# Sliding-window attention with the values stationary, alternating head groups and an early division

## The chip, the cores and the metric

The kernel runs on one core of one Trainium2 chip. The metric is the time of one execution on the device in microseconds (us); lower is better. A core has five engines, each with its own queue of instructions in strict program order: TensorE (PE in the profile; PEld is its weight loads), VectorE (DVE), ScalarE (ACT), GpSimd (POOL) and SyncE (SP, which here issues the loads of weights). They meet only at semaphores: an instruction waits until a counter has reached a value, and another engine's instruction raises that counter.

## The reference

Two layers over 256 tokens of width 1024. Each layer has a mixer (a gated linear recurrence, HGRN2, beside a sliding-window attention), then a dense or an expert MLP, then a gated embedding. The change concerns the attention:

```python
CHUNK = 64; SW_HEADS = 8; KV_HEADS = 2; GROUP = 4; HEAD_DIM = 64; WINDOW = 128

def swa_mixer(q, k, v, q_gain, k_gain, sinks):
    q = rms_norm(q.reshape(B, S, SW_HEADS, HEAD_DIM), q_gain) * HEAD_DIM ** -0.5
    k = rms_norm(k.reshape(B, S, KV_HEADS, HEAD_DIM), k_gain)
    ...
    s = jnp.einsum('bnqhgd,bnkhd->bnhgqk', qb, kb)      # own chunk and the one before
    s = jnp.where(valid, s, -jnp.inf)
    probs = softmax(concatenate([s, sink], -1))[..., :-1]
    o = jnp.einsum('bnhgqk,bnkhd->bnqhgd', probs, vb)
    return o.reshape(B, S, SW_WIDTH)

merged = sigmoid(gate_a) * (ya @ w_pa) + sigmoid(gate_b) * (yb @ w_pb)
x = x + merged @ w_o
```

Everything is float32. Query heads 0 to 3 use key-value head 0, heads 4 to 7 use key-value head 1. The output is (1, 256, 1024).

## The kernel before, in words

**Weights.** All large products are split in two parts for accuracy. A weight unit is 128 x 2048 numbers. SP loads it into one of 6 `raw` slots, ACT writes its high part `w_hi` (L530), DVE its low part `w_lo` (L786), each into one of 3 slots; PE makes three products of it: high by high, low by high, high by low (L1293 to L1295), 512 columns each. `keep_up(used)` on ACT and on DVE splits all units up to number `used + 2`; where it is called decides where in the queue of its engine a unit is split. The units of a mixer are numbered from `base`: 0 to 18 the input projection (`IN_UNITS` = 19; 11 to 18 are the gates, two units to each of `GATES` to `GATES + 3`), 19 and 20 `w_pa`, 21 and 22 `w_pb`, 23 to 26 `w_o`.

**The order of work** is written out by hand for each engine, in three functions named `mixer`, one for ACT, one for DVE and one for PE. No scheduler changes it. The recurrence is done in nine levels: `level_product(g)` on PE, `level_step(g)` on DVE, `level_exp(j)` on ACT. The attention lies between them and between the units of the gates.

**The attention** goes in three tasks, `TASKS`: token tile 0 with all 8 heads, token tile 1 with heads 0 to 3, token tile 1 with heads 4 to 7. Token tile 0 has 128 keys, tile 1 has 256 (the two tiles, masked). Each task fills 1024 columns: 8 heads by 128 keys or 4 by 256. A task goes through these steps:

1. PE, `attention_scores`: one product per head. Both operands lie on 64 partitions, 0 to 63 for heads of group 0 and 64 to 127 for heads of group 1. It raises `sw_scores`.
2. DVE, `softmax_max`: mask, maximum, sink (L921 to L926).
3. ACT, `softmax_exp`: one exponential per head, with its sum (L582 to L585). It raises `sw_probs`.
4. PE, `flip_probs`: 8 transposes of 128 x 128 (L1403).
5. ACT, `take_probs`: a copy into `sw_pT` (L592).
6. PE, `attention_out`: for each head and key block a product with the transposed probabilities stationary (128 x 128) and the values moving (64 columns), so the result has tokens on partitions.
7. DVE, `attention_norm`: sum with the sink, reciprocal (L933, L934), and the multiplication of the result (L937) into `qkv`, which takes the place of the queries. It raises `yb_ready`.

Small products of the attention and of the levels all go through one helper (L1298). Of each such float32 product the trace has two records of PE.

**The end of the mixer.** PE multiplies by the first unit of `w_pa`, then transposes the attention's result by 8 transposes (L1492), then goes on with the second unit of `w_pa`. ACT and DVE split that transposed result into `hT` (L641, L792), PE multiplies by `w_pb`, and DVE merges both branches (L1041 to L1050).

## Time and profile before

| | before |
|---|---|
| median of 3 runs | 1718.02 us (1716.61 to 1719.48) |
| the profiled execution | 1716.82 us, its span 1714.9 us |
| PE, PEld | 1674.0 us (98%), 1389.7 us (81%) |
| DVE, ACT, POOL | 1334.2 us (78%), 1093.1 us (64%), 55.5 us (3%) |
| granted TensorE clock, mean | 0.992 |
| mixer of layer 0, attention part | 101 to 163 us of the span |

Durations of single instructions come from the profiled execution. Its time is 1.2 us below the median, and its span, from the first to the last instruction, 1.9 us below its own time. A busy share is a mean over stages with different limits; whether a saved microsecond counts is read from the waits of the stage in which it lies. Ends of PE instructions are modelled, and one overlaps the next; the time from one start to the next is the better measure. The granted clock is a share of 2.4 GHz; 0.5 is 1.2 GHz.

### The profile page before, as it was taken

The page shows a single profiled execution, that of the slowest core. Times are in us where ns is not written, and L with a number is a line of the kernel's source. Part 1 is how long each engine was busy: PE and PEld are TensorE (multiplying, and loading weights), DVE is VectorE, ACT ScalarE, POOL GpSimd, SP SyncE. Part 2 cuts the span into 40 slices and gives each one's busy share as a digit, 9 for nine tenths or more (in the row PEclk, how much of TensorE's full clock was granted, in tenths as well). Part 3 has the DMA queues.
Part 4 walks back from the last instruction along what each step waited for, and adds up shares of the span by engine and source line. Part 5 has one row for each costly group of instructions (what it writes and reads, how often), then busy time and mean ns, then how long its engine had stood idle before and what let it go on. Part 6 is the DMA issues. An engine that isn't in the chain of part 4 may idle for free.

```text
span 1714.9 us, 20962 instructions
## 1 busy us (share of the span) xinstructions
PE 1674.0 (98%) x7899; PEld 1389.7 (81%) x7899; DVE 1334.2 (78%) x1093; ACT 1093.1 (64%) x897; POOL 55.5 (3%) x52
## 2 busy tenths in 40 slices
PE   7999899999999998999999999999999999999997
PEld 6888788888778887888888888888888888888886
DVE  6785644545567856788988998999998999889885
ACT  5555344344455553777877877778778778778774
POOL 0100000000001000010000000000000000000000
PEclk9999999999999999899999999999999999999999
DMA  8433555565364335599999999999999999999990
GB/s 307 167 123 123 172 172 192 176 196 192 117 213 147 123 123 184 191 363 374 358 380 366 350 383 353 373 377 347 373 385 341 379 377 347 382 377 347 376 370 25
DMA packets 199549, 472.60 MB, mean 276 GB/s; under 512 B 8592, under 2 KB 11216, under 8 KB 199504
## 3 DMA queue, kind: packets, MB, share of 16 engines
q1 hardware_dynamic: 197936, 466.20, 75.6%
q0 software_dynamic: 1568, 5.77, 1.0%
q8 instruction: 32, 0.52, 0.1%
q14 instruction: 13, 0.11, 0.0%
HBM read 469.84 MB, written 2.10 MB: 275 GB/s over the span
## 4 chain that ended last, share of the span: by engine, by line
PE 86%; DVE 9%; issue 3%; ACT 2%; DMA 0%; SPq 0%; DVEq 0%; ACTq 0%
PE ps L1293 26%; PE ps L1295 26%; PE ps L1294 26%; DVE w_lo L786 5%; PE ps L1298 5%; PE ps L1622 1%; ACT w_hi L530 1%; DVE y_lo L1236 1%; DVE hT_lo L792 0%; ACT hT_hi L546 0%; PE ps L1542 0%; PE ps L1403 0%; ACT inner_hi L697 0%; DVE hT_lo L844 0%; PE ps L1384 0%
## 5 line engine op out<-in xcount | busy, mean ns | idle before, releaser
L786 DVE TENSOR_TENSOR w_lo<-raw,w_hi 128x2048 fp32r<-128x2048 f32 x442 | 1007.6, 2290 | 246.7 <-ACT w_hi L530 242.3
L530 ACT ACTIVATE w_hi<-raw 128x2048 fp32r<-128x2048 f32 x442 | 846.5, 1919 | 374.7 <-PE ps L1295 365.1
L1293 PE MATMUL ps<-w_hi,hT_hi 128*128 128x512 f32 (+1 forms) x1600 | 631.2, 394 | 10.9 <-DVE hT_lo L844 4.6
L1295 PE MATMUL ps<-w_hi,hT_lo 128*128 128x512 f32 (+1 forms) x1600 | 621.8, 389 | 0.0
L1294 PE MATMUL ps<-w_lo,hT_hi 128*128 128x512 f32 (+1 forms) x1600 | 621.2, 388 | 0.0
L1293 PEld LDWEIGHTS ps<-w_hi,hT_hi 128*128 128x128 f32 x1600 | 301.7, 189 | 77.3 <-DVE w_lo L786 6.0
L1295 PEld LDWEIGHTS ps<-w_hi,hT_lo 128*128 128x128 f32 x1600 | 301.4, 188 | 63.0
L1294 PEld LDWEIGHTS ps<-w_lo,hT_hi 128*128 128x128 f32 x1600 | 302.0, 189 | 58.8
L1293 PE MATMUL ps<-w_hi,inner_hi 128*128 128x512 f32 x608 | 240.3, 395 | 1.6 <-DVE inner_lo L792 1.6
L1295 PE MATMUL ps<-w_hi,inner_lo 128*128 128x512 f32 x608 | 237.8, 391 | 0.0
L1294 PE MATMUL ps<-w_lo,inner_hi 128*128 128x512 f32 x608 | 237.8, 391 | 0.0
L1293 PEld LDWEIGHTS ps<-w_hi,inner_hi 128*128 128x128 f32 x608 | 114.7, 189 | 26.9 <-DVE inner_lo L792 1.8
L1295 PEld LDWEIGHTS ps<-w_hi,inner_lo 128*128 128x128 f32 x608 | 114.7, 189 | 24.5
L1294 PEld LDWEIGHTS ps<-w_lo,inner_hi 128*128 128x128 f32 x608 | 114.8, 189 | 23.3
L792 DVE TENSOR_TENSOR inner_lo<-ps,inner_hi 128x512 fp32r<-128x512 f32 x72 | 48.8, 685 | 28.4 <-ACT inner_hi L663 14.0
L1298 PE MATMUL ps<-arena 128*128 128x128 f32 (+2 forms) x384 | 50.4, 286 | 1.2 <-DVE arena L937 1.2
L1298 PEld LDWEIGHTS ps<-arena 128*128 128x128 f32 (+1 forms) x384 | 46.9, 191 | 4.3 <-DVE arena L937 1.4
L570 ACT ACTIVATE arena<-ps,rstd 128x512 f32<-128x512 f32 (+1 forms) x40 | 24.4, 661 | 36.8 <-PE ps L1295 36.8
L1206 DVE SCALAR_TENSOR_TENSOR arena<-arena,slot_now,ps 128x512 f32<-128x512 f32 x56 | 41.5, 741 | 0.0
L697 ACT ACTIVATE inner_hi<-ps 128x512 fp32r<-128x512 f32 x56 | 33.1, 591 | 9.9 <-PE ps L1622 9.9
L577 ACT ACTIVATE arena<-arena 128x1024 f32<-128x1024 f32 x16 | 16.7, 1054 | 30.9 <-DVE arena L862 30.9
L1622 PEld LDWEIGHTS ps<-ident,arena 128*128 128x128 f32 x224 | 27.6, 139 | 7.4 <-DVE arena L1206 0.3
(230 smaller groups left out, 776.2 us busy)
## 6 DMA issues: line engine op xcount, KB each, us to landing
raw<-in_w_moe_gate SPq DMA_DIRECT2D x112, 1024.0 KB, 6.9
raw<-in_w_moe_up SPq DMA_DIRECT2D x112, 1024.0 KB, 7.3
raw<-in_w_moe_down SPq DMA_DIRECT2D x112, 1024.0 KB, 6.7
raw<-in_w_in SPq DMA_DIRECT2D x38, 1024.0 KB, 5.6
raw<-in_w_dense_gate SPq DMA_DIRECT2D x14, 1024.0 KB, 5.0
raw<-in_w_dense_up SPq DMA_DIRECT2D x14, 1024.0 KB, 5.1
raw<-in_w_dense_down SPq DMA_DIRECT2D x14, 1024.0 KB, 4.8
raw<-in_w_o SPq DMA_DIRECT2D x8, 1024.0 KB, 4.8
```

The source lines that it names most:

```text
L530: nc.scalar.activation(w_hi[:, n % SLOTS, :], raw[:, n % RAW_SLOTS, :], ACT.Copy).then_inc(high_ready, 1)
L570: nc.scalar.activation(dst(t), src, func, scale=rstd[:, t:t + 1]).then_inc(proj_taken, 1)
L697: nc.scalar.activation(innerT[0][:, :, s % 2 * P:(s % 2 + 1) * P], banks(TRA).rearrange("p (k t) -> p k t", k=4), ACT.Copy).then_inc(item_ ...
L786: nc.vector.tensor_tensor(w_lo[:, n % SLOTS, :], raw[:, n % RAW_SLOTS, :], w_hi[:, n % SLOTS, :].bitcast(F32), ALU.subtract).then_inc(low_ ...
L792: return nc.vector.tensor_tensor(part[1][cols], full, part[0][cols].bitcast(F32), ALU.subtract)
L1206: nc.vector.scalar_tensor_tensor(act[s % 2], act[s % 2], slot_now[:, 0:1], banks(UP), ALU.mult, ALU.mult).then_inc(item_act, 1)
L1236: nc.vector.tensor_tensor(y_lo[:, cols], banks(half), y_hi[:, cols].bitcast(F32), ALU.subtract).then_inc(item_y_split, 1)
L1293: nc.tensor.matmul(o, x_parts[0][x_cols], parts[0], start=first, stop=False)
L1294: nc.tensor.matmul(o, x_parts[0][x_cols], parts[1], start=False, stop=False)
L1295: return nc.tensor.matmul(o, x_parts[1][x_cols], parts[0], start=False, stop=last)
L1298: return nc.tensor.matmul(o, lhsT, rhs, start=start, stop=stop)
L1622: last = nc.tensor.transpose(banks(TRA)[:, k * P:(k + 1) * P], act[s % 2][:, k * P:(k + 1) * P], ident[:, :])
```

## The change

1. `TASKS` now names the heads of each task: task 1 has heads 0, 1, 4, 5 and task 2 heads 2, 3, 6, 7, so each has two heads of either group. `attention_scores` issues a head of group 0, then one of group 1, and so on, each group into its own bank of PSUM.
2. `attention_scale` on DVE takes the sum and the reciprocal and multiplies the probabilities (128 x 1024) before they are transposed; `flip_probs` waits for its semaphore, `sw_scaled`, in place of `sw_probs`.
3. `attention_out` has the values stationary (64 columns) and the probabilities moving (256 columns in task 0, 128 in tasks 1 and 2). The result has head dimensions on partitions, the even head of a pair on 0 to 63 and the odd on 64 to 127: it is already transposed.
4. `take_heads` copies it into the place of the queries. The 8 transposes and `yb_transposed` go; ACT waits for `yb_ready` and for the input projection's end, and ACT and DVE split from SBUF.

```diff
-    TASKS = [(0, 0, 8), (1, 0, 4), (1, 4, 4)]
+    TASKS = [(0, 0, [0, 1, 2, 3, 4, 5, 6, 7]), (1, 0, [0, 1, 4, 5]), (1, 4, [2, 3, 6, 7])]
...
+                act_e.wait_ge(yb_ready, len(TASKS) * (layer + 1))
+                act_e.wait_ge(units_used, base + IN_UNITS)
                 for h in range(2):
-                    act_e.wait_ge(yb_transposed, 2 * layer + h + 1)
-                    nc.scalar.activation(hT[0][:, 2 * h:2 * h + 2, :], banks(GATE + h).rearrange("p (h t) -> p h t", h=2),
-                                         ACT.Copy).then_inc(ybT_high, 1)
+                    nc.scalar.activation(yT(hT[0][:, 2 * h:2 * h + 2, :]), yb[:, 2 * h:2 * h + 2], ACT.Copy).then_inc(ybT_high, 1)
...
-            def attention_norm(layer, a):
+            def attention_scale(layer, a):
...
+                sv = sw_s.rearrange("p (h k) -> p h k", h=heads)
                 dve.wait_ge(sw_probs, len(TASKS) * layer + a + 1)
                 link(nc.vector.tensor_tensor(sw_total[:, hs], sw_sum[:, hs], sw_sink[:, hs], ALU.add))
                 link(nc.vector.reciprocal(sw_recip[:, hs], sw_total[:, hs]))
+                nc.vector.tensor_tensor(sv, sv, sw_recip[:, hs].unsqueeze(2).to_broadcast([P, heads, 1024 // heads]),
+                                        ALU.mult).then_inc(sw_scaled, 1)
+
+            def take_heads(layer, a):
+
                 dve.wait_ge(sw_out, len(TASKS) * layer + a + 1)
...
+                nc.vector.tensor_copy(dst, src).then_inc(yb_ready, 1)
...
                 keep_up(base + 13)
+                attention_scale(layer, 0)
                 level_step(layer, 7)
-                attention_norm(layer, 0)
+                take_heads(layer, 0)
...
                 keep_up(base + 15)
+                attention_scale(layer, 1)
...
-                attention_norm(layer, 1)
+                take_heads(layer, 1)
                 softmax_max(layer, 2)
                 keep_up(base + 16)
+                attention_scale(layer, 2)
                 keep_up(base + 17)
...
             def attention_scores(layer, a):
-                t, h0, heads = TASKS[a]
+                t, _, order = TASKS[a]
                 keys = (t + 1) * P
-                for h in range(h0, h0 + heads):
-                    kv0 = (h // 4) * HEAD_DIM
-                    last = mm(banks(2, 2)[:, (h - h0) * keys:(h - h0 + 1) * keys],
-                              qbT[kv0:kv0 + HEAD_DIM, h % 4, t * P:(t + 1) * P], kbT[kv0:kv0 + HEAD_DIM, 0:keys], True, True)
+                half = len(order) // KV_HEADS
+                for n in range(half):
+                    for v in range(KV_HEADS):
+                        h, slot = order[v * half + n], v * half + n
+                        rows_of = slice(v * HEAD_DIM, (v + 1) * HEAD_DIM)
+                        last = mm(banks(2, 2)[:, slot * keys:(slot + 1) * keys],
+                                  qbT[rows_of, h % 4, t * P:(t + 1) * P], kbT[rows_of, 0:keys], True, True)
                 last.then_inc(sw_scores, 1)
...
-                pe.wait_ge(sw_probs, len(TASKS) * layer + a + 1)
+                pe.wait_ge(sw_scaled, len(TASKS) * layer + a + 1)
...
-                for h in range(heads):
-                    v0 = SW + KV + ((h0 + h) // 4) * HEAD_DIM
+                probs = sw_pT.rearrange("p (b v c j k) -> p b v j c k", b=t + 1, v=KV_HEADS, j=2, k=P)
+                into = banks(OUT_BANK[a]).rearrange("p (v c k) -> p v c k", v=KV_HEADS, c=2)
+                if a:
+                    into = into[:, :, a - 1:a]
+                for v in range(KV_HEADS):
+                    v0 = SW + KV + v * HEAD_DIM
                     for kb in range(t + 1):
-                        last = mm(banks(OUT_BANK[a])[:, h * HEAD_DIM:(h + 1) * HEAD_DIM],
-                                  sw_pT[:, (kb * heads + h) * P:(kb * heads + h + 1) * P],
-                                  qkv[:, kb, v0:v0 + HEAD_DIM], kb == 0, kb == t)
+                        for j in range(2):
+                            last = mm(into[j * HEAD_DIM:(j + 1) * HEAD_DIM, v], qkv[:, kb, v0:v0 + HEAD_DIM],
+                                      probs[:, kb, v, j], kb == 0, kb == t)
                 last.then_inc(sw_out, 1)
...
-                pe.wait_ge(yb_ready, len(TASKS) * (layer + 1))
-                for k in range(4):
-                    for t in range(TILES):
-                        last = nc.tensor.transpose(banks(GATE, 2)[:, k * SEQ + t * P:k * SEQ + (t + 1) * P],
-                                                   qkv[:, t, k * P:(k + 1) * P], ident[:, :])
-                    if k % 2:
-                        last.then_inc(yb_transposed, 1)
```

DVE's queue around the division of task 0, before. `w_lo` is the low part of weight unit 15 (then of unit 16), L886 to L899 are `level_step(7)`, and L933 to L937 are `attention_norm(0)`.

```order
L786 TENSOR_TENSOR w_lo<-raw,w_hi 128x2048 [waits high_ready]
L886 TENSOR_TENSOR arena<-arena 128x4x128 [waits level_exps]
L887 TENSOR_TENSOR arena<-arena 128x4x128
L899 COPY_PREDICATED arena<-masks,ps 128x1024 [waits level_taken,level_scores]
L933 TENSOR_TENSOR sw_total<-sw_sum,sw_sink 128x8 [waits sw_probs]
L934 RECIPROCAL sw_recip<-sw_total 128x8 [waits vector_step]
L937 TENSOR_TENSOR arena<-ps,sw_recip 128x512 [waits sw_out,vector_step]
L786 TENSOR_TENSOR w_lo<-raw,w_hi 128x2048 [waits high_ready]
```

The same place after the change (its lines have other numbers: L791 is the low part, L891 to L904 the level step).

```order
L791 TENSOR_TENSOR w_lo<-raw,w_hi 128x2048 [waits high_ready]
L947 TENSOR_TENSOR sw_total<-sw_sum,sw_sink 128x8 [waits sw_probs]
L948 RECIPROCAL sw_recip<-sw_total 128x8 [waits vector_step]
L949 TENSOR_TENSOR normed<-normed,sw_recip 128x1024 [waits vector_step]
L891 TENSOR_TENSOR arena<-arena 128x4x128 [waits level_exps]
L892 TENSOR_TENSOR arena<-arena 128x4x128
L904 COPY_PREDICATED arena<-masks,ps 128x1024 [waits level_taken,level_scores]
L958 COPY arena<-ps 128x512 [waits sw_out]
L791 TENSOR_TENSOR w_lo<-raw,w_hi 128x2048 [waits high_ready]
```

Sum and reciprocal have moved ahead of the level step, the multiplication has moved with them and is now of the probabilities (`normed` holds them), and all three stand behind the low part of unit 15.

PE's queue from the last level product before the transposes of task 0, before: L1298 is the level product, L1403 the transposes, L1293 the next product of the gates.

```order
L1298 MATMUL ps<-arena 128x128 [waits level_ready,level_taken]
L1298 MATMUL ps<-arena 128x128 x7
L1403 MATMUL ps<-ident,normed 128x128 [waits sw_probs]
L1403 MATMUL ps<-ident,normed 128x128 x7
L1293 MATMUL ps<-w_hi,hT_hi 128x512 [waits low_ready]
```

And after:

```order
L1320 MATMUL ps<-arena 128x128 [waits level_ready,level_taken]
L1320 MATMUL ps<-arena 128x128 x7
L1429 MATMUL ps<-ident,normed 128x128 [waits sw_scaled]
L1429 MATMUL ps<-ident,normed 128x128 x7
L1315 MATMUL ps<-w_hi,hT_hi 128x512 [waits low_ready]
```

Nothing has moved; the semaphore of the wait is another one.

PE's queue at `attention_out(0)` and the scores of task 1, before. The products of 64 columns are the results, the four of 128 columns a level product, those of 256 the scores.

```order
L1298 MATMUL ps<-arena,normed 128x64 [waits sw_pT_ready]
L1298 MATMUL ps<-arena,normed 128x64 x7
L1298 MATMUL ps<-arena 128x128 [waits level_ready,level_taken]
L1298 MATMUL ps<-arena 128x128 x3
L1298 MATMUL ps<-arena 128x256 [waits yb_ready]
L1298 MATMUL ps<-arena 128x256 x3
```

And after:

```order
L1320 MATMUL ps<-normed,arena 64x256 [waits sw_pT_ready]
L1320 MATMUL ps<-normed,arena 64x256 x3
L1320 MATMUL ps<-arena 128x128 [waits level_ready,level_taken]
L1320 MATMUL ps<-arena 128x128 x3
L1320 MATMUL ps<-arena 128x256 [waits yb_ready]
L1320 MATMUL ps<-arena 128x256 x3
```

Eight products of 64 columns have become four of 256 that write 64 partitions each. The scores have the same shapes; their partitions alternate, which these rows do not show.

## Rows read from the trace of the kernel before

**Rows 1.** The page, busy time, share and instructions of PE, PEld, DVE, ACT.

```profile
PE 1674.0 (98%) x7899; PEld 1389.7 (81%) x7899; DVE 1334.2 (78%) x1093; ACT 1093.1 (64%) x897; POOL 55.5 (3%) x52
```

**Rows 2.** The page, the chain that ended last, shares of the span by engine.

```profile
PE 86%; DVE 9%; issue 3%; ACT 2%; DMA 0%; SPq 0%; DVEq 0%; ACTq 0%
```

**Rows 3.** The chain in order of time: start us, us, what. Layer 0.

```profile
155.06 1.73 PE ps L1298 x16
...
162.34 0.87 PE ps L1492 x8
```

**Rows 4.** PE in time: start us, us, engine, line, operation, count, [idle before].

```profile
101.27 1.71 PE L1298 MATMUL ps<-arena 64*128 64x128 f32 x16
...
110.28 1.95 PE L1298 MATMUL ps<-arena 128*128 128x128 f32 x16
...
112.07 1.04 PE L1403 MATMUL ps<-ident,normed 128*128 128x128 f32 x8
...
131.35 1.04 PE L1403 MATMUL ps<-ident,normed 128*128 128x128 f32 x8
...
140.16 1.99 PE L1298 MATMUL ps<-arena 64*128 64x256 f32 x8 [0.59 <-DVE arena L937]
...
148.54 1.04 PE L1403 MATMUL ps<-ident,normed 128*128 128x128 f32 x8
...
171.31 0.19 PEld L1293 LDWEIGHTS ps<-w_hi,hT_hi 128*128 128x128 f32 x1 [0.34 <-DVE w_lo L786]
...
583.64 1.04 PE L1403 MATMUL ps<-ident,normed 128*128 128x128 f32 x8
```

**Rows 5.** DVE in time, layer 0.

```profile
114.09 2.29 DVE L786 TENSOR_TENSOR w_lo<-raw,w_hi 128x2048 fp32r<-128x2048 f32 x1 [2.01 <-ACT w_hi L530]
116.30 0.68 DVE L886 TENSOR_TENSOR arena<-arena 128x512 f32<-128x512 f32 x1
...
118.69 0.15 DVE L933 TENSOR_TENSOR sw_total<-sw_sum,sw_sink 128x8 f32<-128x8 f32 x1
118.89 0.20 DVE L934 RECIPROCAL sw_recip<-sw_total 128x8 f32<-128x8 f32 x1
...
126.66 2.28 DVE L786 TENSOR_TENSOR w_lo<-raw,w_hi 128x2048 fp32r<-128x2048 f32 x1
132.61 1.22 DVE L1008 TENSOR_REDUCE head_sumsq<-arena 128x8 f32<-128x1024 f32 x1 [3.67 <-ACT arena L626]
...
145.06 2.28 DVE L786 TENSOR_TENSOR w_lo<-raw,w_hi 128x2048 fp32r<-128x2048 f32 x1
...
176.88 1.23 DVE L1050 TENSOR_TENSOR arena<-arena 128x1024 f32<-128x1024 f32 x1
```

**Rows 6.** ACT in time, layer 0.

```profile
111.21 1.04 ACT L577 ACTIVATE arena<-arena 128x1024 f32<-128x1024 f32 x1
112.16 1.90 ACT L530 ACTIVATE w_hi<-raw 128x2048 fp32r<-128x2048 f32 x1
...
155.68 0.68 ACT L570 ACTIVATE arena<-ps,rstd 128x512 f32<-128x512 f32 x1
156.25 1.91 ACT L530 ACTIVATE w_hi<-raw 128x2048 fp32r<-128x2048 f32 x1
...
162.81 1.09 ACT L641 ACTIVATE hT_hi<-ps 128x512 fp32r<-128x512 f32 x2 [4.64 <-PE ps L1492]
```

**Rows 7.** DVE in time, the place of layer 1 that answers to 114.09.

```profile
585.68 2.29 DVE L786 TENSOR_TENSOR w_lo<-raw,w_hi 128x2048 fp32r<-128x2048 f32 x1 [2.01 <-ACT w_hi L530]
```

**Rows 8.** PE, L1298 by stretches: stretch, length, busy (records), clock, DMA share, GB/s.

```profile
101.70:102.15 0.45, 0.45 (x9) 1.00 0.89 355
...
103.05:103.50 0.45, 0.45 (x5) 1.00 0.95 391
```

**Rows 9.** By stretches: length, PE, PEld, DVE, ACT, POOL busy (instructions), granted clock.

```profile
185.00:188.30 3.30, 3.15 (x8) 2.49 (x9) 3.30 (x5) 1.68 (x1) 0.00 (x0) 0.51 0.82 237
...
656.60:663.00 6.40, 6.28 (x15) 4.97 (x16) 4.05 (x5) 1.65 (x1) 1.64 (x3) 0.52 0.90 262
```

More of the change, by code:

```diff
@@ L200, in build_trunk, with yT @@
         level_tile = [deep[:, (3 + n) * 1024:(4 + n) * 1024] for n in range(2)]
+        yb = qkv[:, :, 0:SW].rearrange("p t (m k) -> p m t k", k=P)
+        def yT(heads):
+            return heads.rearrange("p m (t k) -> p m t k", k=P)
         att = normed.rearrange("p t n -> p (t n)")
@@ L336, in build_trunk @@
         sw_probs = sem("sw_probs")
+        sw_scaled = sem("sw_scaled")
         sw_probs_transposed = sem("sw_probs_transposed")
@@ L579, in softmax_exp @@
                 def softmax_exp(a):
[L580 removed]
+                    h0, heads = TASKS[a][1], len(TASKS[a][2])
                     act_e.wait_ge(sw_max_ready, tasks + a + 1)
@@ L913, in softmax_max @@
             def softmax_max(layer, a):
-                t, h0, heads = TASKS[a]
+                t, h0, order = TASKS[a]
+                heads = len(order)
                 dve.wait_ge(sw_scores, len(TASKS) * layer + a + 1)
@@ L1029, in mixer @@
                 keep_up(base + 18)
-                attention_norm(layer, 2)
+                take_heads(layer, 2)
                 keep_up(base + 19)
@@ L1033, in mixer @@
                     dve.wait_ge(ybT_high, 2 * layer + h + 1)
-                    last = low(hT, banks(GATE + h).rearrange("p (h t) -> p h t", h=2), (slice(None), slice(2 * h, 2 * h + 2)))
+                    last = nc.vector.tensor_tensor(yT(hT[1][:, 2 * h:2 * h + 2, :]), yb[:, 2 * h:2 * h + 2],
+                                                   yT(hT[0][:, 2 * h:2 * h + 2, :]).bitcast(F32), ALU.subtract)
                 last.then_inc(ybT_ready, 1)
```

36 lines of the change are left out of this document (19 added, 17 removed).

## The prediction

> **What bounds the kernel now.** I read first the busy shares of the engines [rows 1] and the shares of the chain of waits [rows 2], then the same chain in order of time around the attention of layer 0 [rows 3], then the instructions in time of TensorE (PE), VectorE (DVE) and ScalarE (ACT) there, and last the granted clock. PE is busy 98% of the span and holds 86% of the chain: work taken from PE shortens the kernel, and so does nothing else unless PE waits for it. In the attention, from 101 to 163 us in layer 0, the reader is to see PE instructions back to back; the one wait is 0.59 us in front of the scores of task 2 [rows 4]. DVE and ACT have idle time, but DVE is a queue in strict order, and its place in that order is what the change touches. Layer 1 repeats layer 0, 471.6 us later: its copy of unit 15 of the weights starts on DVE at 585.68, that of layer 0 at 114.09 [rows 5, 7]. So I work out one layer and double it.
>
> **Part 1: the division ahead of the transposes (the loss).** Before, `flip_probs` waits for the exponentials of ACT. Now it waits for `sw_scaled`, a multiplication of all 128x1024 probabilities on DVE. For task 0 it stands behind `keep_up(base + 13)`, the low part of weight unit 15. That low part needs ACT's high part, which ACT issues only behind the eight exponentials and `level_exp(7)`: 111.21 and 1.04 us, then the copy at 112.16 of 1.90 us [rows 6]. DVE takes it at 114.09, after 2.01 us idle, and has its next instruction at 116.30 [rows 5]. None of this hangs on what the change saves on PE: ACT's exponentials follow DVE, which has no idle time in the 12 us before those 2.01. Behind it come the sum and the reciprocal, 0.20 us from start to start (118.69 to 118.89), so 0.40 for both, and the multiplication. The trace has no multiplication of this shape by a broadcast row; the nearest is another two-operand instruction on 128x1024 in SBUF, 1.23 us (176.88) [rows 5]. Bounds: 0.68 us, what 128x512 takes (116.30), and double the 1.23, 2.46. I take 1.23, the same size in the same memory. So `sw_scaled` comes at 116.30 + 0.40 + 1.23 = 117.93. The transposes started at 112.07 [rows 4]: PE is 5.9 us later. Queued behind the waiting transpose are the second half of a gate projection, `attention_out(0)` and everything else of PE. Layer 1 gives the same: unit 15 starts at 585.68, hence 2.21 us later the next instruction and 589.5 for `sw_scaled`, against transposes at 583.64 [rows 4].
>
> PE arrives at the wait even earlier, because the scores of task 0 get shorter (below), and is idle some 6.4 us. What idle does to the clock the trace shows behind two waits of 1.7 and 1.9 us near the end of each mixer: the granted clock was 0.51 over the next 3.3 us in layer 0 and 0.52 over 6.4 us in layer 1 [rows 9], the lower level of 1.2 GHz, which cost 0.49 x 3.3 = 1.6 us and 0.48 x 6.4 = 3.1 us. A longer wait should do it too. I take 1.7 us, near the smaller, as part of the low stretch lies in the idle time itself; bounds 0 and 3.1. The Trainium skill, "TensorE: Matmul & The Clock Gate", section "Why this matters for your kernels", says that idle gaps between bursts of matmuls put the clock back to its lower level. It agrees with these rows and speaks against this change.
>
> For task 1 DVE is done with `keep_up(base + 15)` at 126.66 + 2.28 = 128.94 and then waited 3.67 us for ACT's squares (132.61) [rows 5]. The division needs 1.63 us there: ready at 130.57. The transposes started at 131.35 [rows 4], but scores that are 0.8 us shorter bring PE there at 130.55: 0 to 0.1 us of wait. For task 2: `keep_up(base + 16)` starts at 145.06 and takes 2.28, so 147.34 + 1.63 = 148.97, against transposes at 148.54 [rows 4, 5]: 0.45 us of wait. DVE's start there follows the end of the scores of task 2, so PE's gain before that does not change it.
>
> **Part 2: heads of the two groups alternately (a gain).** A score contracts over 64 partitions: 0 to 63 for the first group, 64 to 127 for the second. In task 0 before, there is one change from one to the other in the middle of 8 products (16 records, two to a product), and there the trace shows overlap: 9 records of PE in the 0.45 us from 101.70, against 5 in 0.45 us of the full-height products behind it [rows 8]. Alternating, each record has a partner of the other half. Task 0 took 1.7 us from 101.27 [rows 4]; a full overlap makes it 1.1. This gain of 0.6 goes into the wait of part 1 and is worth nothing. Tasks 1 and 2 had four heads of one group each, with no partner: 8 records of 256 columns in 1.99 us (140.16) [rows 4]. Now half of them lie beside the other half: 1.0 and a start of 0.15, 1.15 us. Gain 0.8 each; bounds 0 and 1.0.
>
> **Part 3: values stationary (a gain, less sure).** `attention_out` had 8 products (16 records) of 64 moving columns over full 128-column weights, 1.73 us (155.06, task 2) [rows 3]. Now task 0 has 4 products of 256 columns, 8 records; in sequence that is the 1.99 us of the row above. Tasks 1 and 2 have 8 products of 128 columns, 16 records, each at the pace of the level products, of which 16 begin at 110.28 and are over when the transposes start at 112.07 [rows 4], 1.79 us. So in sequence nothing is gained, or 0.2 is lost. But one head of a pair writes partitions 0 to 63 and the other 64 to 127, from weights only 64 columns wide. No row here shows whether two such products overlap. By the nearest rows, the overlap of the halves in part 2, they do: 1.1 us, a gain of 0.65 each; bounds a loss of 0.2 and a gain of 0.8. In task 2 ACT sets an end: the projection behind needs ACT's last copy of the gates, 155.68 + 0.68 = 156.36 [rows 6], while the results were over at 155.06 + 1.73 = 156.79 [rows 3]. So at most 0.43 of its 0.65 arrives; I take 0.3.
>
> The Trainium skill, the same page, section "Part 3: Packing small matmuls — row/col tiling", says that matmuls whose outputs lie in different column groups run beside each other. "TensorEngine Tiling (Array Packing)", section "Key Properties", sets against it that a change of tiling mode drains the engine. By the first alone the figures of this part stand; if each change cost as much as was saved, the second rival below would hold.
>
> **Part 4: no transposes of the result (a gain).** The 8 transposes between the two units of `w_pa` go, 0.87 us of the chain [rows 3]. ACT and DVE now split from SBUF. ACT waited for those transposes until 162.81; now it can do so from 156.25 + 1.91 = 158.2, when it has copied unit 21 [rows 6]. Its sigmoid and the high part of unit 22 behind it come earlier, and the wait of 0.34 us for that unit at 171.31 goes as well [rows 4]. I take 1.2 together. Next in line is the same merge as before. The copies out of `attention_out` read as much as the multiplications did: no change.
>
> **The sum.** Per layer: 5.9 + 1.7 for the wait and its clock; against it 0.65 (out 0), 0.8 - 0.1 (scores 1), 0.65 (out 1), 0.8 - 0.45 (scores 2), 0.3 (out 2), 1.2 (part 4) = 3.85. Net 3.75 slower, 7.5 for two layers. The profiled execution took 1716.82 us, its span 1714.9; so 1724.3, or 0.44% more. The median of the runs is 1.2 us above it: 1725 for the number to compare. What can be told from no change here is about 0.2%, 3.4 us.
>
> **Rivals.**
> *The column halves do not overlap.* Part 3 gives 0 in place of 1.6 per layer: 3.2 more, 1728. For it: no row shows such overlap. Against: the row halves do it. If the start of the new shape costs 0.2 each time, 1729.
> *The clock holds.* After the wait it returns at once, or falls inside the idle time: 2 x 1.7 less, 1721.5. With a low stretch as that of layer 1 it is 2 x 1.4 more, 1728. Against the first: both stretches of [rows 9] came after shorter waits. The stretches at the ends of the mixers may also move, by 1 to 3 us either way.
> *The division is covered, and the kernel is faster.* Place: the first division of each layer; price 5.9 + 1.7. It decides if `sw_scaled` comes before PE has ended the level products, at 111.5. Then all of PE's savings count, 3.85 + 0.6 per layer, twice that from 1718: 1709. It would need DVE to divide before unit 15, or ACT to split that unit before its exponentials; the order on both engines is as said.
> *The wait is shorter than the gains.* With the multiplication at 0.68 us, the clock held and every overlap at its upper bound (5.3 against 4.8 per layer), it ends 1 us above before, 1719: no change that can be measured.
>
> **How the numbers follow.** Forecast as summed 0.55; column halves in sequence 0.17; clock held or shorter 0.17; wait as short as the gains 0.07; division covered 0.04. Faster by over 0.2%, under 1714.6: 0.05. Within 0.2%, up to 1721.5: half of the clock rival and the short wait, with some of the forecast's own spread, 0.15. Slower: 0.80. The range is 1719 to 1731: from the clock held with good overlap to no overlap of columns with a long low stretch.
>
> **What would show it.** In the profile after: a wait of PE for DVE of some 6 us in front of the first transposes of probabilities in each layer (none before); small waits, 0 to 0.5 us, in front of the second and third; a granted clock near one half behind the first. Scores of tasks 1 and 2 in about 1.1 us, results in about 1.1 us (1.8 if the columns do not overlap). No PE wait at the last unit of `w_pb`. It is wrong if PE waits under 4 us at the first transposes, or if the time is under 1718.

## The result, and the profile after

| | before | after |
|---|---|---|
| median of 12 runs each | 1717.84 us (1715.42 to 1719.96) | 1722.38 us (1718.30 to 1727.33) |
| ratio | | 1.0026, interval 1.0013 to 1.0038 |
| the profiled execution, its span | 1716.82, 1714.9 us | 1718.30, 1716.4 us |
| granted clock, mean | 0.992 | 0.993 |

The change makes the kernel slower by 0.26%, 4.5 us between the medians, where 7.5 were forecast (7 between the medians). The profiled execution is the fastest of the twelve. The runs of after lie in two groups: 1718.3 to 1723.1 us at a mean clock of 0.991 to 0.993, and 1725.1 to 1727.3 at 0.988 to 0.989. So part of the time goes with the clock and not with the work.

The page of after, busy time (line 1, against [rows 1]) and the chain's shares (line 2, against [rows 2]):

```profile
PE 1661.1 (97%) x7867; PEld 1374.5 (80%) x7867; DVE 1341.8 (78%) x1099; ACT 1093.4 (64%) x897; POOL 53.4 (3%) x52
...
PE 81%; DVE 11%; issue 3%; ACT 3%; POOL 1%; DMA 0%; SPq 0%; DVEq 0%; ACTq 0%
```

PE is busy 12.9 us less and the kernel is not faster: 5% of the chain has gone from PE to other engines. The waits of after between 84 and 190 us (engine, operand, line, releaser: us in total, times, longest) name the place:

```profile
PE ps L1429 <- DVE normed L949: 6.7, 2, 6.4
```

PE in time in layer 0 of after, the places of [rows 4] (start us, us, engine, line, operation, count, [idle before]):

```profile
101.23 3.14 PE L1320 MATMUL ps<-arena 64*128 64x128 f32 x32
...
117.98 1.97 PE L1429 MATMUL ps<-ident,normed 128*128 128x128 f32 x8 [6.35 <-DVE normed L949]
...
126.39 1.08 PE L1320 MATMUL ps<-normed,arena 128*64 128x256 f32 x8
127.40 2.22 PE L1320 MATMUL ps<-arena 128*128 128x128 f32 x16
...
129.55 0.50 PE L1315 MATMUL ps<-w_hi,hT_hi 128*128 128x512 f32 x1
...
137.84 1.04 PE L1429 MATMUL ps<-ident,normed 128*128 128x128 f32 x8
...
145.91 1.14 PE L1320 MATMUL ps<-arena 64*128 64x256 f32 x8 [0.53 <-DVE arena L958]
146.97 0.50 PE L1315 MATMUL ps<-w_hi,hT_hi 128*128 128x512 f32 x1
...
153.97 1.09 PE L1429 MATMUL ps<-ident,normed 128*128 128x128 f32 x8 [0.37 <-DVE normed L949]
...
160.48 1.09 PE L1320 MATMUL ps<-normed,arena 128*64 128x128 f32 x16
161.95 0.47 PE L1315 MATMUL ps<-w_hi,inner_hi 128*128 128x512 f32 x1 [0.38 <-issue]
```

DVE in time behind the low part of unit 15, and the second merge of the mixer, against [rows 5]:

```profile
114.06 2.29 DVE L791 TENSOR_TENSOR w_lo<-raw,w_hi 128x2048 fp32r<-128x2048 f32 x1 [2.02 <-ACT w_hi L535]
116.27 0.16 DVE L947 TENSOR_TENSOR sw_total<-sw_sum,sw_sink 128x8 f32<-128x8 f32 x1
116.46 0.20 DVE L948 RECIPROCAL sw_recip<-sw_total 128x8 f32<-128x8 f32 x1
116.70 1.23 DVE L949 TENSOR_TENSOR normed<-normed,sw_recip 128x1024 f32<-128x1024 f32 x1
...
184.02 1.22 DVE L1071 TENSOR_TENSOR arena<-arena,ps 128x1024 f32<-128x1024 f32 x1 [2.89 <-PE ps L1317]
```

The low part starts at 114.06 as before (114.09), the multiplication takes 1.23 us, and the transposes start at 117.98, where 117.93 was forecast. Before, the places in which the prediction counts its gains started as follows; the last row is the second merge:

```profile
118.40 1.89 PE L1298 MATMUL ps<-arena,normed 128*128 128x64 f32 x16
...
123.09 0.50 PE L1293 MATMUL ps<-w_hi,hT_hi 128*128 128x512 f32 x1
...
142.09 0.50 PE L1293 MATMUL ps<-w_hi,hT_hi 128*128 128x512 f32 x1
...
154.90 1.89 PE L1298 MATMUL ps<-arena,normed 128*128 128x64 f32 x16
156.60 0.48 PE L1293 MATMUL ps<-w_hi,inner_hi 128*128 128x512 f32 x1
```

```profile
179.81 1.22 DVE L1049 TENSOR_TENSOR arena<-arena,ps 128x1024 f32<-128x1024 f32 x1 [1.71 <-PE ps L1295]
```

Subtracting start from start gives how far after lags at each place, and the change from one place to the next gives each term of the sum:

| place, layer 0 | before | after | lag | term | forecast |
|---|---|---|---|---|---|
| transposes, task 0 | 112.07 | 117.98 | 5.91 | wait +5.9 | +5.9 |
| results, task 0 | 118.40 | 126.39 | 7.99 | clock +2.1 | +1.7 |
| first product behind the scores of task 1 | 123.09 | 129.55 | 6.46 | -1.53 | -1.45 |
| transposes, task 1 | 131.35 | 137.84 | 6.49 | 0 | +0.1 |
| first product behind the scores of task 2 | 142.09 | 146.97 | 4.88 | -1.61 | -1.45 |
| transposes, task 2 | 148.54 | 153.97 | 5.43 | +0.55 | +0.45 |
| `w_pa`, first unit | 156.60 | 161.95 | 5.35 | -0.1 | -0.3 |
| second merge | 179.81 | 184.02 | 4.21 | -1.14 | -1.2 |

The mixer is thus 4.2 us longer up to its second merge, against 3.75 forecast. If nothing else had happened, the kernel would be 8.4 us slower. What else happened is seen in the stretches around both ends of the mixers (length, then PE, PEld, DVE, ACT, POOL busy with their instructions, then the granted clock, the DMA share and GB/s). Before:

```profile
178.00:200.00 22.00, 18.59 (x83) 15.10 (x82) 11.84 (x11) 9.60 (x8) 0.00 (x0) 0.92 0.50 160
...
649.00:679.00 30.00, 26.59 (x113) 21.60 (x112) 15.36 (x12) 11.52 (x9) 2.91 (x4) 0.89 0.57 184
679.00:720.00 41.00, 38.71 (x197) 32.95 (x196) 30.18 (x66) 27.49 (x32) 2.85 (x4) 0.88 0.42 149
```

After, with the stretches behind the two first transposes:

```profile
113.00:125.00 12.00, 7.02 (x27) 5.98 (x28) 6.21 (x7) 3.85 (x3) 0.00 (x0) 0.72 0.27 87
178.00:200.00 22.00, 18.59 (x90) 15.23 (x89) 13.98 (x11) 7.69 (x7) 0.00 (x0) 1.00 0.44 143
588.00:600.00 12.00, 7.66 (x29) 6.53 (x30) 6.21 (x7) 3.21 (x3) 0.00 (x0) 0.72 0.26 87
649.00:679.00 30.00, 26.59 (x125) 21.87 (x124) 19.16 (x14) 11.91 (x10) 2.91 (x4) 1.00 0.58 183
679.00:720.00 41.00, 38.71 (x203) 32.73 (x203) 28.93 (x66) 27.57 (x32) 2.85 (x4) 0.92 0.44 147
```

The low clock has moved: it is now behind the waits for the division, and no longer at the ends of the mixers. Before, PE's first product behind the end of the mixer took 0.80 us, after 0.50, although the wait ahead of it is the same 1.71 us. The first line is of before, the second of after:

```profile
185.15 0.80 PE L1293 MATMUL ps<-w_hi,hT_hi 128*128 128x512 f32 x1 [1.71 <-DVE hT_lo L792]
```

```profile
189.36 0.50 PE L1315 MATMUL ps<-w_hi,hT_hi 128*128 128x512 f32 x1 [1.71 <-DVE hT_lo L797]
```

What that gave back is read from ACT's first split behind each end. Layer 0, and layer 1, before:

```profile
203.30 1.92 ACT L530 ACTIVATE w_hi<-raw 128x2048 fp32r<-128x2048 f32 x1 [3.52 <-PE ps L1295]
...
676.20 1.92 ACT L530 ACTIVATE w_hi<-raw 128x2048 fp32r<-128x2048 f32 x1 [3.52 <-PE ps L1295]
```

After:

```profile
206.07 1.92 ACT L535 ACTIVATE w_hi<-raw 128x2048 fp32r<-128x2048 f32 x1 [3.52 <-PE ps L1317]
...
680.45 1.92 ACT L535 ACTIVATE w_hi<-raw 128x2048 fp32r<-128x2048 f32 x1 [3.52 <-PE ps L1317]
```

The lag falls from 4.21 to 2.77 at the end of layer 0 (1.44 given back). The second layer adds its 4.25 (2.77 + 4.25 = 7.02), and its end gives 2.77 back: 4.25 at 680.45. Behind that another 2.75 go until the spans end 1.5 us apart. The higher clock of 679 to 720 accounts for 41 x 0.04 = 1.6 of them. Before also had 3.4 us of low clock between 1679 and 1684, which after has not; how much of the last 1.1 us that is, the rows do not show. Read in steps of 1 us up to PE's last product, the low clock adds up to 23.9 us before and 20.5 after: it has moved more than it has shrunk.

### The profile page after: what moved, and what is told of

It reads as the page before. It is cut to its first block, busy times and chain, and to the rows that moved or that the text cites. A ratio compares the mean times of both kernels' runs of the same rounds, so it can differ in the third digit from the quotient of the medians.

```text
span 1716.4 us, 20900 instructions
## 1 busy us (share of the span) xinstructions
PE 1661.1 (97%) x7867; PEld 1374.5 (80%) x7867; DVE 1341.8 (78%) x1099; ACT 1093.4 (64%) x897; POOL 53.4 (3%) x52
## 4 chain that ended last, share of the span: by engine, by line
PE 81%; DVE 11%; issue 3%; ACT 3%; POOL 1%; DMA 0%; SPq 0%; DVEq 0%; ACTq 0%
PE ps L1315 25%; PE ps L1317 25%; PE ps L1316 25%; DVE w_lo L791 5%; PE ps L1320 3%; PE ps L1646 1%; ACT w_hi L535 1%; ACT normed L590 1%; DVE y_lo L1258 1%; DVE hT_lo L797 0%; PE ps L1429 0%; POOL head_rstd L488 0%; DVE arena L904 0%; ACT hT_hi L551 0%; PE ps L1566 0%
## 5 line engine op out<-in xcount | busy, mean ns | idle before, releaser
L791 DVE TENSOR_TENSOR w_lo<-raw,w_hi 128x2048 fp32r<-128x2048 f32 x442 | 1007.6, 2290 | 237.4 <-ACT w_hi L535 232.9
L1320 PE MATMUL ps<-arena 128*128 128x128 f32 (+2 forms) x384 | 45.9, 287 | 1.1 <-DVE arena L958 1.1
L1320 PEld LDWEIGHTS ps<-arena 128*128 128x128 f32 (+1 forms) x384 | 42.9, 191 | 4.6 <-DVE arena L958 1.5
```

Of the source, the lines that this page charges most:

```text
L791: nc.vector.tensor_tensor(w_lo[:, n % SLOTS, :], raw[:, n % RAW_SLOTS, :], w_hi[:, n % SLOTS, :].bitcast(F32), ALU.subtract).then_inc(low_ ...
L1320: return nc.tensor.matmul(o, lhsT, rhs, start=start, stop=stop)
```

## The experiments

Two quantities are compared. The time is the median of runs, with its ratio to the kernel before and the interval. The *mixer stretch* is that of layer 0 from the start of the scores of task 0 to the second merge: before 179.81 - 101.27 = 78.54 us, after 184.02 - 101.23 = 82.79. The theory: the wait for the division and the low clock behind it cost 8 us a layer, the packing of products gives some 4 back. The main rival: the new shapes of the products, not the wait, cost the time. The experiments were compared in several groups, each with runs of the kernel before beside it, whose median was 1717.6 to 1718.0.

**The changed kernel again.** No edit.

> The changed kernel once more, beside the others of this job, as their measure. Theory (the division's wait in each layer and the low TensorE clock behind it, against shorter products): 1718 to 1727 us as before, median near 1722, 4 to 5 us above the kernel before. If its time hangs on where low-clock stretches fall elsewhere in the program, the runs with a mean granted clock near 0.993 are at 1718 to 1721 and those near 0.989 at 1724 to 1727.

1720.43 us over 12 runs (1718.35 to 1724.77), ratio 1.0014, interval 1.0003 to 1.0026; the kernel before beside it 1717.97 over 29 runs. Mixer stretch 82.95, wait 6.36. Slower again, by 2.5 us where the first comparison gave 4.5. Part of that is the clock: in the first comparison five of twelve runs had a mean clock of 0.988 or 0.989, here one. It is not all: the nine runs at 0.993 still lie between 1718.35 and 1721.86. The two traces agree in the mixer, but here the attention starts 1.0 us later (102.25, not 101.23), because the first transfer that PE waits for came later (10.80, not 9.77).

**The division alone.** On the kernel before:

```diff
 keep_up(base + 13)
+attention_scale(layer, 0)      # sum, reciprocal, probabilities times it
 level_step(layer, 7)
-attention_norm(layer, 0)
+take_heads(layer, 0)           # a plain copy; tasks 1 and 2 alike
...
-pe.wait_ge(sw_probs, len(TASKS) * layer + a + 1)
+pe.wait_ge(sw_scaled, len(TASKS) * layer + a + 1)
```

> The kernel before with only the division put ahead of the transposes, at the same places on VectorE; heads, orientation of the result and its transposes as before. Theory: the wait of the first transposes costs 5.9 us and the low clock behind it 2.1, the third transposes wait 0.45 us, and nothing is gained: 8.4 us per layer, the second merge multiplication of layer 0 starts at 188.2 instead of 179.8 us, and the time is about 1734 us (1731 to 1738). Rival, that the wait costs little because PE's later work is ahead of its operands anyway: under 1727 us.

1731.12 us over 6 runs (1728.72 to 1731.93), ratio 1.0075, interval 1.0057 to 1.0092. Mixer stretch 88.62:

```profile
102.25 3.69 PE L1307 MATMUL ps<-arena 64*128 64x128 f32 x32
...
119.01 1.97 PE L1412 MATMUL ps<-ident,normed 128*128 128x128 f32 x8 [5.80 <-DVE normed L937]
```

The wait is 5.80 us, shorter than the 6.35 of the changed kernel by what its quicker scores of task 0 take (3.69 against 3.14 us for those records). So the gain in those scores is worth nothing, as forecast, and the division costs 13 us when nothing pays for it. This is the largest effect of any part, and with the old shapes in place it can't be that of the new ones. The stretch grew by 10.1 us where 8.4 were expected. The rest is mostly clock: it was low once more in it, 0.50 from 151.7 to 155.1 us, 1.7 us at half speed.

**The alternation alone.** On the kernel before, `TASKS` keeps its form and a list gives the heads:

```diff
+    ORDER = [[0, 1, 2, 3, 4, 5, 6, 7], [0, 1, 4, 5], [2, 3, 6, 7]]
...
-                for h in range(h0, h0 + heads):
+                half = heads // KV_HEADS
+                for n in range(half):
+                    for v in range(KV_HEADS):
+                        h, slot = ORDER[a][v * half + n], v * half + n
```

Sinks, values and the copies of the result follow the list.

> The kernel before with only the heads regrouped and issued alternately; division behind, probabilities stationary, transposes of the result kept. Theory: the row halves overlap, the three scores get shorter by 0.6, 0.85 and 0.85 us per layer, nothing waits longer: 2.3 us per layer, the second merge multiplication of layer 0 starts at 177.5 us, time about 1713 us (1710 to 1716), faster than before. Rival, that the next wait takes the gain back (the transposes of task 2 then wait for the exponentials): the scores are shorter but the time is that of before.

1712.0 us over 12 runs, ratio 0.9954, interval 0.994 to 0.9969. Mixer stretch 76.24, so 2.3 less. The scores of tasks 1 and 2 took 1.99 us [rows 4] and now:

```profile
138.68 1.13 PE L1310 MATMUL ps<-arena 64*128 64x256 f32 x8 [0.58 <-DVE arena L952]
```

The stretch explains 4.6 us, the median fell by 6.0. The spans of the traces are 9.6 apart (1714.9 and 1705.3): 4.6 and half of the 10.2 us by which the low clock up to PE's last product is shorter (23.9 and 13.7) make 9.7. Its runs are of two kinds, five at 1705.6 to 1707.1 with a mean clock of 0.995 to 0.997 and seven at 1711.9 to 1713.6 with 0.992 or 0.993: the same instructions, some 6 us apart, and the clock with them.

**Work in the wait.** In the changed kernel, 24 products of the identity, which nothing reads, between the last level product and the transposes of task 0:

```diff
                 level_product(layer, 7)
+                pe.wait_ge(level_taken, layer * (LEVEL_COUNT + 1) + 7)
+                for n in range(24):
+                    mm(banks(GATE)[:, 0:P], ident[:, :], ident[:, :], True, True)
```

> The changed kernel with 24 products of the identity by itself (128x128, float32, 5.4 us) into an unused bank between the last level product and the first transposes of each layer, so that PE is not idle in the wait; they change no result. Theory: PE waits no less for the division (the transposes start at 118.0 us as in the changed kernel), but the granted clock behind it stays at 1.0, the second half of the gate projection takes 5.5 us instead of 6.8 and the second merge multiplication of layer 0 starts near 181.9 instead of 184.0 us. 2.1 us less per layer up to there; the low stretches at the ends of the mixers may come back and take 1.6 to 3.1 us each, so the whole is 1718 to 1722 us. Rival, that the clock behind the wait is not what costs the 2 us: the merge stays at 184.0 us.

1717.38 us over 12 runs, ratio to the kernel before 0.9999, interval 0.9987 to 1.0012, beside 1720.43 without the filler: 3.05 us less by adding work. That is a little below the 1718 to 1722 expected. PE in time, then the two stretches behind the first transposes:

```profile
114.29 5.62 PE L1320 MATMUL ps<-ident 128*128 128x128 f32 x48 [0.47 <-DVE arena L904]
120.18 1.09 PE L1429 MATMUL ps<-ident,normed 128*128 128x128 f32 x8 [0.26 <-DVE normed L949]
...
126.67 1.08 PE L1320 MATMUL ps<-normed,arena 128*64 128x256 f32 x8
```

```profile
113.00:125.00 12.00, 11.27 (x82) 10.20 (x81) 7.47 (x9) 6.06 (x8) 0.00 (x0) 1.00 0.26 89
...
588.00:600.00 12.00, 11.73 (x80) 9.94 (x78) 6.23 (x7) 4.27 (x5) 0.00 (x0) 1.00 0.25 89
```

From the first transposes to the results of task 0 it is now 6.49 us, where it was 8.41 (126.39 - 117.98): the low clock behind the wait costs 1.9 us a layer, and the mixer stretch is 80.88, 2.07 shorter than the 82.95 above. That makes 4.1 us for two layers. The spans are only 2.9 apart (1717.8 and 1714.9) because in this trace the attention starts 1.2 us later (103.42, not 102.25), for a reason that the repetitions below show. A low stretch came back at the end of the second mixer (clock 0.94 from 649 to 679, in after 1.00), but the one behind it got shorter (0.96 from 679 to 720, in after 0.92). The two are about equal.

**The two column halves one after the other.** In the changed kernel:

```diff
-                for v in range(KV_HEADS):
-                    v0 = SW + KV + v * HEAD_DIM
-                    for kb in range(t + 1):
-                        for j in range(2):
+                for j in range(2):
+                    for v in range(KV_HEADS):
+                        v0 = SW + KV + v * HEAD_DIM
+                        for kb in range(t + 1):
```

> The changed kernel with the results' products in another order: all of the even heads (partitions 0 to 63), then all of the odd ones. Theory: only the two products at the change of halves overlap, so the results take about 1.7 us instead of 1.05 each, 0.6 us more in tasks 0 and 1 and 0.3 in task 2, 1.5 us per layer, 3 us in all, 1722 to 1727 us. Rival, that two products of different halves go side by side whatever their order: no difference in the profile.

1721.57 us over 10 runs, ratio 1.0018, interval 1.0008 to 1.0029, just below the 1722 to 1727 expected; mixer stretch 83.23. PE in time, the results of tasks 0, 1 and 2:

```profile
126.40 1.09 PE L1320 MATMUL ps<-normed,arena 128*64 128x256 f32 x8
...
144.31 1.58 PE L1320 MATMUL ps<-normed,arena 128*64 128x128 f32 x16
...
160.97 1.58 PE L1320 MATMUL ps<-normed,arena 128*64 128x128 f32 x16
```

Half right. With eight products of 128 columns the order matters, 1.58 us against 1.09. With four of 256 it does not: two products of the even heads are issued before two of the odd, and they still took 1.09. That the order matters at all shows that products of different halves run beside each other. Whether the four are spared by their number or by their longer columns, and how PE does it, no run shows. The effect on the whole is 0.4 us of stretch, and is not told apart by the time.

**The division ahead of the low part.** In the changed kernel, DVE's order:

```diff
-                keep_up(base + 13)
                 attention_scale(layer, 0)
+                keep_up(base + 13)
```

> The changed kernel with one call moved on VectorE: the division of task 0 stands ahead of keep_up(base + 13), the split of unit 15. Theory: VectorE is free at 112.0 us, so the probabilities are divided at 113.7 and the first transposes start there instead of at 118.0; PE waits 2.1 us in place of 6.4, the clock behind it mostly stays up, and unit 15 is needed only 7 us later. 4.3 to 6.4 us less per layer up to the second merge multiplication (near 178 to 179.7 us in layer 0), time about 1712 us (1708 to 1716), below both kernels. Rival, that the exponentials or something else hold the transposes: they start at 116 us or later and the time stays above 1717.

1708.26 us over 6 runs (1705.68 to 1710.65), ratio to the kernel before 0.9939, interval 0.9924 to 0.9954: 9.4 us faster than before, 12 to 14 faster than the two medians of after, which come from other groups of runs. The wait fell from 6.35 to 2.02, the mixer stretch to 78.14. In layer 1 the same stretch, from 573.26 to 649.81, is 76.55, and before it was 78.54 there as well. So the stretches give 0.4 and 2.0 us; most of the rest of the 9.4 is clock, at the ends of the mixers, as its repetition below shows.

**The projection ahead of the transposes.** In the changed kernel DVE's order is kept and PE is given other work first:

```diff
                 level_product(layer, 7)
-                flip_probs(layer, 0)
                 project(GATES + 1, 1)
-                attention_out(layer, 0)
+                flip_probs(layer, 0)
                 level_product(layer, 8)
+                attention_out(layer, 0)
```

> The changed kernel with PE's order changed and nothing else: the second half of the second gate projection ahead of the first transposes of probabilities, and the last level product ahead of the first results. Theory: PE works 5.5 us of its 6.4 us wait away, transposes start at 118.0 as in the changed kernel but with the projection done; the second merge multiplication of layer 0 at about 177 us, time about 1708 us (1704 to 1712). Rival, that the later copy of the transposed probabilities on ScalarE and the split of unit 16 behind it then hold PE: a wait of PE for low parts of some us behind the scores of task 1, time above 1714.

1709.08 us over 5 runs, ratio 0.9945, interval 0.993 to 0.9959; mixer stretch 76.75:

```profile
120.86 1.09 PE L1429 MATMUL ps<-ident,normed 128*128 128x128 f32 x8 [0.91 <-DVE normed L949]
...
125.09 1.13 PE L1320 MATMUL ps<-arena 64*128 64x256 f32 x8 [0.80 <-DVE arena L958]
```

The wait can be taken away from either side: 0.91 us are left of it, and 0.80 at the scores of task 1. The wait for low parts that the rival expected is not there.

**Both.** 

> Both moves: the division of task 0 ahead of the split of unit 15 on VectorE, and the gate projection ahead of the first transposes on PE. Theory: the probabilities are ready at 113.7, before PE comes to the transposes at 117, so no wait is left there; about 0.9 us per layer less than with PE's order alone, time about 1707 us (1703 to 1711). Rival: no difference from PE's order alone, because the wait left there is under 1 us and the next end (the copy of the probabilities on ScalarE) is the same.

1709.40 us over 5 runs, ratio 0.995, interval 0.9935 to 0.9966; no wait at the first transposes, mixer stretch 75.55, the shortest of all. Yet the time is that of either move alone, as the rival expected, if for another reason: the 1.2 us per layer gained in the stretch lie below what moves from run to run (1707.75 to 1711.71 here).

**The clock in repetitions.** One more trace each: the kernel before (twice), the changed kernel, and the changed kernel with the division ahead of the low part. No new edits.

> The kernel before, profiled again. Question: is the low-clock stretch at the end of each mixer (3.4 us in layer 0, 6.8 us in layer 1 of its first profile) a property of this kernel, or does it come and go from one execution to the next? Theory, that it comes and goes: its place and length differ here, and the stretch from the first scores to the second merge multiplication is 78.5 us again. Rival, a property: low behind both mixers again, 3 to 7 us each.

> The kernel before, profiled a third time, to the same question. Theory: at least one of the two profiles lacks one of the two low stretches, and their times differ by about half of the difference in low time. Rival: both have both.

> The changed kernel with the division of task 0 ahead of the split of unit 15, profiled again. Its mixer is only 0.4 us shorter than that of the kernel before, its time 9 us. Theory: the rest is granted clock, lower in the kernel before for some 30 us of the span and here for about 16; again no low stretch behind either mixer, and a wait of 2.0 us in front of the first transposes. Rival: low stretches behind the mixers as in the first profile of before, and then a time near 1713.

> The changed kernel, profiled a third time. Theory: the 6.8 us of low clock behind the wait of the first transposes are there in both layers each time, since the wait is 6.4 us; the stretches at the ends of the mixers come and go. Rival: the low stretch behind the wait comes and goes as well, in one layer at least.

They took 1719.98, 1717.42, 1706.06 and 1719.06 us, one run each. The granted clock by stretches, all traces of the three kernels (three of before; three of after, the first two being those above; two of the division first):

| stretch, us | before | after | division first |
|---|---|---|---|
| 113 to 125, behind the first transposes | 1.00, 1.00, 1.00 | 0.72, 0.72, 0.72 | 0.86, 1.00 |
| 178 to 200, end of mixer 0 | 0.92, 0.84, 0.92 | 1.00, 1.00, 1.00 | 1.00, 1.00 |
| 588 to 600, the same in layer 1 | 1.00, 1.00, 1.00 | 0.72, 0.72, 0.72 | 1.00, 1.00 |
| 649 to 679, end of mixer 1 | 0.89, 0.89, 0.89 | 1.00, 1.00, 1.00 | 1.00, 1.00 |
| 679 to 720 | 0.88, 0.88, 0.88 | 0.92, 0.92, 0.92 | 0.92, 0.92 |

Behind the wait of 6.4 us the clock was low every time. Behind the waits of 1.7 us at the ends of the mixers it was low in every trace of before and in none of after. So the theory that those stretches come and go failed for both kernels: their place is a property of the kernel, and only the length varied (6.8 us at the end of mixer 0 in the second trace of before, 3.4 in the other two). Behind the wait of 2.0 us of the division first it was low in one of four places, layer 0 of the first trace:

```profile
115.95 1.19 PE L1429 MATMUL ps<-ident,normed 128*128 128x128 f32 x8 [2.02 <-DVE normed L949]
```

and not in the second:

```profile
113.83 1.09 PE L1429 MATMUL ps<-ident,normed 128*128 128x128 f32 x8 [2.02 <-DVE normed L949]
```

The mixer stretch of the second is 76.55 (177.96 - 101.41), of the first 78.14: 1.6 us of clock. With 76.55 the gain of this kernel over before adds up, if the ends of the mixers give what they give in after: 2.0 a layer makes 4, the ends 1.4 + 2.8, the clock from 679 to 720 another 1.6, in sum 9.8 of the 10.7 us between the spans (1714.9 and 1704.2).

The two traces of this kernel are 3.6 us apart, and the clock is only part of it. The attention starts at 103.54 in the first and at 101.41 in the second, with the clock at 1.00 up to there in both. The difference lies in one instruction of GpSimd, whose result DVE and then PE wait for; first trace, then second:

```profile
76.77 4.59 POOL L486 TENSOR_SCALAR head_meansq<-head_sumsq 128x20 f32<-128x20 f32 x1 [54.05 <-DVE head_sumsq L992]
```

```profile
76.75 2.18 POOL L486 TENSOR_SCALAR head_meansq<-head_sumsq 128x20 f32<-128x20 f32 x1 [54.04 <-DVE head_sumsq L992]
```

Together 2.1 us here and 1.6 in the mixer stretch make up the 3.6. The instruction took 4.59 us in four of the 14 traces (division first, work in the wait, projection first, both moves) and 2.18 in the others; in layer 1 it took 2.18 in all. Why is not shown. A difference of 2 us between two single spans can be this and nothing of the change.

Even the same instructions of one kernel can run at either clock. The second and the third trace of before, behind the same wait of 1.19 us at the start of layer 1's mixer:

```profile
488.58 0.80 PE L1293 MATMUL ps<-w_hi,hT_hi 128*128 128x512 f32 x1 [1.19 <-DVE hT_lo L844]
```

```profile
487.58 0.50 PE L1293 MATMUL ps<-w_hi,hT_hi 128*128 128x512 f32 x1 [1.19 <-DVE hT_lo L844]
```

**All kernels together**

| kernel | median, us | ratio to before | mixer stretch, us |
|---|---|---|---|
| before | 1717.6 to 1718.0 | | 78.54, 78.55, 78.57 |
| after | 1722.4, 1720.4 | 1.0026, 1.0014 | 82.79, 82.95, 83.13 |
| division alone | 1731.1 | 1.0075 | 88.62 |
| columns one after the other | 1721.6 | 1.0018 | 83.23 |
| work in the wait | 1717.4 | 0.9999 | 80.88 |
| alternation alone | 1712.0 | 0.9954 | 76.24 |
| both moves | 1709.4 | 0.9950 | 75.55 |
| projection first | 1709.1 | 0.9945 | 76.75 |
| division first | 1708.3 | 0.9939 | 78.14, 76.55 |

The stretches are those of layer 0. Four versions beat both kernels; between the best three the runs do not decide, and their intervals overlap that of the fourth.

## Why the prediction was right, and what it mis-sized

*The wait of part 1* was right to 0.05 us, in place and in cause. Reading DVE's queue, with the low part of unit 15 waiting for ACT, gave the start of the transposes; taking the division out of that queue position took the wait from 6.35 to 2.02 us. Of the signs that were named, the waits at the second and third transposes came as said (none and 0.37 us), and PE had no wait at the last unit of `w_pb`.

*The low clock behind it* was taken as 1.7 us a layer and measured 2.1 by the lag, 1.9 to 2.1 by the filler. It was inside the bounds of 0 and 3.1. The reason given for a value near the smaller holds: the clock was low from about 115.2 to 122.0, and until 117.98 PE was idle. The prediction cited the Trainium skill on idle gaps, "TensorE: Matmul & The Clock Gate", section "Why this matters for your kernels"; for the long wait every trace agrees (0.72 in six of six stretches). For waits of 1 to 2 us the rows show both, low and not, so there the rule does not decide.

*The gains of parts 2 to 4* were 3.85 and measured 3.8 (7.99 - 4.21). The least sure term, the column halves, came out as taken: behind the results of task 0 the next product starts after 1.01 us (126.39 to 127.40), where in sequence they would need 1.99 by the estimate of the prediction. The first rival, no overlap, falls. A full overlap of those 1.99 makes 1.00, so what the new shape costs at its start is small: the last product ahead of it starts at 126.07, 0.32 us before it, where before it was 0.23 (118.17 to 118.40). The Trainium skill, "TensorEngine Tiling (Array Packing)", section "Key Properties", says that such a change drains the engine; of its cost this trace shows at most the 0.1 us between the two. (The prediction says that a dear change would make its second rival; it is the first one that it would make.) Only the results of task 2 gave 0.1 in place of 0.3. The prediction took their old end from the modelled 156.79, but the product behind them started at 156.60, so ACT's copy at 156.36 left 0.24 to gain, not 0.43; in after that copy ends at 161.85 and PE starts at 161.95.

*What failed* is one term. "The stretches at the ends of the mixers may also move, by 1 to 3 us either way" stood in a rival, was given no sign, and was left out of the sum. They did move, both of them and in every trace: 1.44 + 2.77 = 4.2 us given back, and some 1.6 more before 720. With them the sum would have been 4.2 x 2 - 4.2 = 4.2 us slower. That it is near the 4.5 and 2.5 of the medians is in part chance: in the two traces from which it is read the 1.6 and another 1.1 go as well, and 1.5 are left. Why the clock holds at the ends of the mixers in the changed kernel stays open. The wait there is the same 1.7 us. What differs is the work before it (the packed products, the transposes that are gone) and when it comes. The alternation alone, with the old results and their transposes, is enough to bring 1.00 there. It isn't the earlier low stretch at the division that protects it: the kernels with the alternation alone, with both moves and with the division first had 1.00 at the end of the first mixer with no low stretch, or almost none, before. With the division alone, the old shapes, it was 0.92, and with the columns in sequence too. No experiment here separates these.

*The rivals.* The one with the division covered (1709 us) was turned down because DVE's order excludes it; with that order changed, the kernel takes 1708.3. Its condition was read rightly, but that its number fits is luck. It counted 8.9 us of savings on PE in the mixers. With the division first the stretches of the two layers gave 0.4 + 2.0 in one trace and 4.0 in the other, and with both moves, where no wait is left at the first transposes, 3.0 a layer. The rest came from the clock at the ends of the mixers and behind them, which that rival did not count. The last rival, the wait as short as the gains, has a sum that cannot be done again: with the division 0.55 us shorter, the upper bounds of parts 2 and 3 with the 1.2 of part 4 give 0.8 + 1.0 + 0.8 + 1.0 + 0.43 + 1.2 = 5.2 and not 4.8 against its 5.3. It would end nearer to before, with the same verdict.

## What to carry to other kernels

Before moving an operation to the front of a chain, look at what stands ahead of it in its engine's queue, and place it ahead of the instruction that itself waits for another engine; here one moved line is the difference between 0.26% slower and 0.6% faster, part of it by way of the clock. Test the parts of a bundled change apart: here the alternation was a gain, the early division a loss, and both were hidden in a near-zero sum. Count the clock with every wait added on TensorE, also at the places which the change does not touch, and read a difference of a few us against the mean granted clock of the runs and against where the changed stage starts in each trace.

## What was not expected of the hardware

- Products in different column halves overlapped as well when their order did not alternate, with four products of 256 columns (1.09 us in either order), and only partly with eight of 128 (1.58 against 1.09).
- Adding 5.6 us of useless products in front of a wait made the changed kernel 3 us faster.
- The same instructions behind the same wait ran at either clock level from one execution to the next, and one kernel's runs fell in two groups 6 us apart (1705.6 to 1707.1 and 1711.9 to 1713.6 us) with mean clocks of 0.995 to 0.997 and 0.992 to 0.993.
- One small GpSimd instruction (128x20) took 4.59 us in four of 14 traces and 2.18 in ten, and moved everything behind it by 2.1 us.
